# Second attention's probabilities: turned by 32x32 block transposes and a trip through device memory instead of by TensorE

## The reference, cut to what matters

```python
s = jnp.einsum('bnqhgd,bnshd->bnhgqs', q, kb).astype(jnp.float32) * HEAD_DIM ** -0.5 + bias
s = jnp.where(mask[None, :, None, None], s, -jnp.inf)
p = jax.nn.softmax(jnp.concatenate([s, sink], axis=-1), axis=-1)[..., :-1]
o = jnp.einsum('bnhgqs,bnshd->bnqhgd', p.astype(vb.dtype), vb)
return o.reshape(B, S, N_HEADS * HEAD_DIM) @ w_out
```

## Time and profile before

| | us |
|---|---|
| median of 3 runs | 2210.76 (2210.42 to 2211.42) |
| span of the profiled execution | 2209.0 |
| its own total | not listed apart from the three runs |
| TensorE busy | 2197.2 |
| VectorE busy | 1445.2 |
| ScalarE busy | 1106.9 |
| GpSimd busy | 550.7 |

### The profile page before, as it was taken

The page is one execution under the profiler, slowest core; times in us unless marked ns, Lnnn a source line. Parts: engine busy times, 40 slices in busy tenths (PEclk is TensorE's granted clock), DMA queues, the critical chain, the costliest instruction groups (busy, mean ns, idle before and its releaser), DMA issues.

```text
span 2209.0 us, 34195 instructions
## 1 busy us (share of the span) xinstructions
PE 2197.2 (99%) x11625; PEld 1878.9 (85%) x11625; DVE 1445.2 (65%) x1925; ACT 1106.9 (50%) x1654; POOL 550.7 (25%) x531
## 2 busy tenths in 40 slices
PE   9999999999999999999999999999999999999998
PEld 7888988888888888888888887888888888888887
DVE  6877765555664565555566667567785688756875
ACT  6445555453453454445455455565553455534553
POOL 3202220350240141053000033005540245403431
PEclk9999999999999999999999999999999999999999
DMA  7675335556555555556555653545555555555554
GB/s 254 232 230 163 115 128 204 170 190 208 191 190 192 189 189 192 186 192 193 187 185 179 227 171 135 193 160 188 195 188 196 192 183 192 189 195 192 186 209 149
DMA packets 118072, 414.21 MB, mean 188 GB/s; under 512 B 12896, under 2 KB 18048, under 8 KB 117472
## 3 DMA queue, kind: packets, MB, share of 16 engines
q1 hardware_dynamic: 111600, 401.37, 53.9%
q10 hardware_dynamic: 6384, 11.70, 1.7%
HBM read 409.29 MB, written 2.15 MB: 186 GB/s over the span
## 4 chain that ended last, share of the span: by engine, by line
PE 98%; DVE 1%; ACT 1%; issue 0%; DMA 0%; DVEq 0%; ACTq 0%
PE bank L486 33%; PE bank L494 17%; PE bank L543 7%; PE bank L545 7%; PE bank L544 7%; PE bank L1059 4%; PE bank L1060 4%; PE bank L1061 4%; PE bank L599 1%; PE bank L601 1%; PE bank L600 1%; PE bank L619 1%; PE bank L994 1%; PE bank L656 1%; PE bank L796 1%; PE bank L798 1%
## 5 line engine op out<-in xcount | busy, mean ns | idle before, releaser
L1100 DVE TENSOR_TENSOR wboth<-raw,wboth 128x1024 fp32r<-128x1024 f32 x756 | 982.2, 1302 | 607.8 <-ACT wboth L1802 607.1
L1802 ACT CAST wboth<-raw 128x1024 fp32r<-128x1024 f32 x756 | 790.9, 1049 | 711.5 <-PE bank L545 241.6
L486 PE MATMUL bank<-A,wboth 128*128 128x512 f32 x2928 | 705.1, 391 | 0.3 <-DVE wboth L1100 0.3
L486 PEld LDWEIGHTS bank<-A,wboth 128*128 128x128 f32 x2928 | 537.0, 188 | 104.6 <-issue 1.0
L494 PEld LDWEIGHTS bank<-A,wboth 128*128 128x128 f32 x2928 | 376.7, 191 | 14.8
L494 PE MATMUL bank<-A,wboth 128*128 128x256 f32 x2928 | 384.0, 283 | 0.0
L543 PE MATMUL bank<-wboth,H 128*128 128x512 f32 x576 | 224.6, 390 | 0.0
L545 PE MATMUL bank<-wboth,H 128*128 128x512 f32 x576 | 224.2, 389 | 0.0
L544 PE MATMUL bank<-wboth,H 128*128 128x512 f32 x576 | 224.1, 389 | 0.0
L2257 POOL TENSOR_TENSOR bias<-z,rs 128x256 f32<-128x256 f32 x64 | 75.7, 1182 | 481.2 <-DVE z L1131 391.6
L2257 POOL TENSOR_TENSOR PT<-z,rs 128x256 f32<-128x256 f32 x88 | 73.4, 835 | 465.4 <-DVE z L1131 464.8
(11 more groups left out here) (293 smaller groups left out, 2409.1 us busy)
## 6 DMA issues: line engine op xcount, KB each, us to landing
raw<-wstream SPq DMA_DIRECT2D x756, 512.0 KB, 3.3
bias<-bias_rows ACTq DMA_DIRECT2D x6, 512.0 KB, 5.4
x<-xrows ACTq DMA_DIRECT2D x1, 2048.0 KB, 10.0
bias<-grows ACTq DMA_DIRECT2D x2, 1024.0 KB, 6.1
out<-x SPq DMA_DIRECT2D x8, 256.0 KB, 2.1
x<-xT SPq DMA_DIRECT2D x7, 256.0 KB, 4.6
pA<-bias_rows ACTq DMA_DIRECT2D x2, 512.0 KB, 8.9
Sm<-grows ACTq DMA_DIRECT2D x1, 1024.0 KB, 5.8
```

The lines of the kernel that those rows point to most:

```text
L486: last = nc.tensor.matmul(bank(j)[:, :], whi[:, s, cols(i)], moving(j, k), start=(k == 0), stop=(k == K - 1))
L1100: V.tensor_tensor(wlo[:, s, :], raw[:, s, :], whi[:, s, :].bitcast(F32), ALU.subtract).then_inc(lo_ready, 1)
L1802: C.copy(whi[:, s, :], raw[:, s, :]).then_inc(hi_ready, 1)
```

## The change

The eight TensorE transposes of a block and the two copies from PSUM go. In their place, at the step where the copies stood, VectorE transposes the block's 128x1024 elements in 32x32 squares from `Sm` into one buffer `flip` (half of `kT`, free by then), ordered so that each group of 32 partitions holds rows that belong together. SyncE stores the buffer to device memory, 512 KB, waits for that to land, and fetches it back in four transfers of 128 KB, each to 32 partitions in runs of 256 elements, into one of two halves of `PT`. There the keys are on partitions, and the output matmuls read the probabilities as runs of 32 columns. SyncE does the store ahead of weight load s + 7 and the fetch ahead of load s + 8 of the stream, s being the step of the flip. The outputs move from places 10, 13, 15 to 13, 16, 18 (last pair: from 34, 36, 37 to 37, 39, 40), "hi" and "lo" with them. A flip waits until the block before has been stored; a fetch waits until the output of the block two before is done. The output projection's first 16 pieces come in another order: rows 0 to 3 of both halves, then 4 and 5 of both, then 6 and 7 of both. The bytes stored and fetched are 1 MB for each of 12 blocks.

```diff
-SWA_AT = {"score": (5, 8, 10), "turn": (9, 12, 14), "out": (10, 13, 15), "max": (6, 9, 11), "exp": (6, 9, 11), "inv": (8, 11, 13),
-          "copy": (10, 13, 15), "hi": (None, 14, 16), "lo": (None, 15, 17)}
...
+SWA_AT = {"score": (5, 8, 10), "max": (6, 9, 11), "exp": (6, 9, 11), "inv": (8, 11, 13), "flip": (10, 13, 15), "out": (13, 16, 18),
+          "hi": (None, 17, 19), "lo": (None, 18, 20)}
+SWA_AT_LAST = {"score": (29, 32, 33), "max": (30, 33, 34), "exp": (30, 33, 34), "inv": (32, 35, 35), "flip": (34, 36, 37),
+               "out": (37, 39, 40), "hi": (None, 40, 41), "lo": (None, 40, 41)}
...
+WO2_FIRST = [(f, h) for hs in ((0, 1, 2, 3), (4, 5), (6, 7)) for f in range(2) for h in hs]
+FLIP_LOAD = 7
...
+    flipped = nc.dram_tensor("flipped", [3 * PAIRS, P, 8 * P], F32).ap()
...
+        flip = kT[:, 1, :, :].rearrange("p a b -> p (a b)")[:, 0:8 * P]
...
+        def swa_probs_of(n, kt, half):
+            t = SWA_BLOCKS[n % 3][0]
+            runs = PT[:, n % 2, :, :].rearrange("p a b -> p (a b)").rearrange("p (i e b) -> p e i b", i=4, e=8)
+            return runs[:, half::2, :, :] if t == 0 else runs[:, 2 * half + kt::4, :, :]
...
+            def swa_store(n):
+                sp.wait_ge(swa["flipped"], n + 1)
+                sp.dma_start(flipped[n], flip).then_inc(swa["stored"], 16)
+            def swa_fetch(n):
+                sp.wait_ge(swa["stored"], 16 * n + 16)
+                if n >= 2:
+                    sp.wait_ge(swa["o_done"], n - 1)
+                for j in range(4):
+                    rows = flipped[n].rearrange("(i a) (j c) -> j a i c", i=4, j=4)[j]
+                    sp.dma_start(PT[32 * j:32 * j + 32, n % 2, :, :].rearrange("p a b -> p (a b)").rearrange("p (i c) -> p i c", i=4),
+                                 rows).then_inc(swa["landed"], 16)
...
+            loads(BLK, first)
+            for i in range(first, last):
+                for n in swa_due("flip", i - PB["q2"] - FLIP_LOAD - 1):
+                    swa_fetch(n)
+                for n in swa_due("flip", i - PB["q2"] - FLIP_LOAD):
+                    swa_store(n)
+                load_one(i)
+            loads(last, NPIECE // SLOTS * SLOTS)
...
-            def swa_turn(n):
-                _, t, _, _, probs = swa_block(n)
-                pe.wait_ge(swa["scaled"], n + 1)
...
-                pe.wait_ge(swa["pt_act"], n + 1)
+                pe.wait_ge(swa["landed"], 64 * n + 64)
...
-                                                PT[:, kt, e0 + half:e1:2, :], start=(kt == 0), stop=(kt == t))
+                                                swa_probs_of(n, kt, half), start=(kt == 0), stop=(kt == t))
...
-            for i, (f, h) in enumerate(WO_FIRST):
+            for i, (f, h) in enumerate(WO2_FIRST):
...
+            def swa_flip(n):
+                dve.wait_ge(swa["scaled"], n + 1)
+                if n:
+                    dve.wait_ge(swa["stored"], 16 * n)
+                V.transpose(flip.rearrange("p (j e b) -> p e j b", j=4, e=8),
+                            Sm[:, n % 3 * 8 * P:(n % 3 + 1) * 8 * P].rearrange("p (e j a) -> p e j a", e=8, j=4)).then_inc(swa["flipped"], 1)
```

More of the change, by code:

```diff
@@ L334, in program @@
             "scores", "max", "step", "shift", "sinkdiff", "exp", "sinkexp", "inverse", "scaled",
-            "turned", "pt_act", "pt_dve", "o_done", "o_hi", "o_ready")}
+            "flipped", "stored", "landed", "o_done", "o_hi", "o_ready")}
         bias_in = [sem(f"bias_in{i}") for i in range(4)]
@@ L436, in load, with loads, load_one @@
                 sp.dma_start(raw[:, s, :], wstream[ds(i, 1)].rearrange("a p n -> p (a n)")).then_inc(raw_landed[s], 16)
[L438 to L441, removed]
+            def loads(a, b):
+                with sp.Fori(a // SLOTS, b // SLOTS) as it:
+                    for j in range(SLOTS):
+                        load(it * SLOTS + j, j)
+            def load_one(i):
                 sp.wait_ge(lo_ready, i - SLOTS + 1)
                 sp.dma_start(raw[:, i % SLOTS, :], wstream[i]).then_inc(raw_landed[i % SLOTS], 16)
+            def swa_store(n):
[9 more added lines that the diff above has]
+                                 rows).then_inc(swa["landed"], 16)
+            first, last = PB["q2"] // SLOTS * SLOTS, (PB["q2"] + ATT_PIECES + FLIP_LOAD) // SLOTS * SLOTS
+            loads(BLK, first)
[6 more added lines that the diff above has]
+            loads(last, NPIECE // SLOTS * SLOTS)
+            for i in range(NPIECE // SLOTS * SLOTS, NPIECE):
+                load_one(i)
             for t in range(QT):
@@ L902, in swa_output @@
                         last = nc.tensor.matmul(psum[4 + t][c, e0 // 2 * P:e1 // 2 * P], vN[:, kt, g * P + half * HD:g * P + half * HD + HD],
[L903 to L905 removed]
+                                                swa_probs_of(n, kt, half), start=(kt == 0), stop=(kt == t))
+                last.then_inc(swa["o_done"], 1)
             def swa_after(i):
@@ L910, in swa_after @@
                     swa_output(n)
-                for n in swa_due("turn", i):
-                    swa_turn(n)
                 for n in swa_due("score", i):
@@ L1630, in _ @@
             for i in range(ATT_PIECES + 2):
-                for n in swa_due("copy", i):
-                    swa_copy(n)
+                for n in swa_due("flip", i):
+                    swa_flip(n)
                 for n in swa_due("lo", i):
@@ L2123, in square @@
                 else:
-                    act.wait_ge(piece_used, SLOTS + PB["wo2"] + (WO_FIRST.index((f, 7)) + 1 if f < 2 else 8 * f + 8))
+                    act.wait_ge(piece_used, SLOTS + PB["wo2"] + (WO2_FIRST.index((f, 7)) + 1 if f < 2 else 8 * f + 8))
                 if f:
@@ L2408, with rows_out @@
     misc = np.concatenate([gates, a["nsa_cmp_w2_k"][0], a["nsa_cmp_w2_v"][0]], axis=1)
-    def rows_out(w):
+    def rows_out(w, order_of):
         by_piece = rows(w).reshape(4, BLK, BLK, P, P)
-        first, half = zip(*WO_FIRST)
+        first, half = zip(*order_of)
         return np.concatenate([by_piece[list(first), list(half)], by_piece[2:].reshape(-1, BLK, P, P)]).reshape(-1, P, P)
     stream = [rows(vs), tiled(kc), tiled(vc), tiled(ks), tiled(kw), in_turn, misc.reshape(P, BLK, P).transpose(1, 0, 2),
-              tiled(w_in[:, :D]), rows_out(a["nsa_w_out"][0])]
+              tiled(w_in[:, :D]), rows_out(a["nsa_w_out"][0], WO_FIRST)]
     for c in range(FF_CHUNKS):
@@ L2426 @@
     sinks = a["swa_sinks_2"][0].reshape(PAIRS, 2, HPG).transpose(0, 2, 1).reshape(-1)
-    stream += [rows(swa[:, D + kv2:]), tiled(swa[:, D:D + kv2]), tiled(swa[:, :D][:, heads]), rows_out(a["swa_w_out_2"][0][heads])]
+    stream += [rows(swa[:, D + kv2:]), tiled(swa[:, D:D + kv2]), tiled(swa[:, :D][:, heads]), rows_out(a["swa_w_out_2"][0][heads], WO2_FIRST)]
     up, down = a["ffn_w_up_2"][0], a["ffn_w_down_2"][0]
```

23 lines of the change are left out of this document (5 added, 18 removed).

## The result

The changed kernel takes 2214.57 us (median of 16 executions, 2211.76 to 2218.81), the kernel before 2211.08 us (16 executions, 2210.34 to 2212.49): a ratio of 1.0017 [1.0010, 1.0024]. It is 3.5 us slower, inside the 4.4 us that were taken as no change, and 2.6 us above the range of the prediction. The profiled execution took 2212.75 us with a span of 2210.9, which answers to the 2209.0 of before.

A forecast was written before the change was run, and what follows sets the result against it. TensorE, busy 99% of the span, was taken to bound the kernel. Removed turns of 9.6 us less a 1.2 us wait gave 8.4 us off, a forecast of 2202.4 us, range 2200.6 to 2212.

The forecast's parts named there:

- The prize: On TensorE, removing 96 turns, twelve groups of eight at about 0.80 us each, saves 9.6 us.
- The turn: On VectorE, one 128x1024 transpose per block takes 1.3 us, ends 0.7 and 2.6.
- The trip in the traffic: Per block, transpose 1.3, store 3.3, fetch 4.2 and hand-overs 0.3 us: 9.1 us, ends 6.9 and 16.4.
- The trip of 9.1 fits in all of them: Covers before the output groups, 10.3 to 13.5 us, hide the trip; only block 11 waits, 1.2 us.
- Rival A: Late landings: trip 11.9 us, 6.5 us of TensorE waits, 3.1 us gained, 2207.6 us; chance 0.20.
- The places: Where TensorE waits for fetched data: block 11 alone, 1.2 us; block 10 has 10.3 us of cover.
- What moves at no cost: Later output groups, 32-column operand runs and the projection's new order cost TensorE zero; output groups stay 1.01 us.
- rival C: 32-column runs slow output groups: prize gone from 1.8 us a group, 2207 us at 1.4; chance 0.08.
- The clock: A lower granted clock after a wait, listed only as a sign of being wrong, with no size.
- The queue: SyncE's in-order queue: weight loads about 3 us late, 8.5 us to spare, hidden until the trip nears 15 us.
- rival B: Slower: output groups wait on fetches, prize spent at a trip of about 12.7 us, 2217 at 14; chance 0.14.

The follow-up runs named there:

- run without a trip: Changed kernel with VectorE transposing straight into `PT`, no store or fetches, probabilities turned only within 32x32 squares: 2201.62 us, ratio 0.9958.
- filled waits: Changed kernel with 8 and 16 matmuls that nothing reads ahead of the waits of blocks 3 and 10: 2212.60 us, ratio 1.0007.
- gain rows later: Changed kernel with the 1 MB gain-row load issued at step 42, after the last fetch landed, not at step 38: 2211.75 us, ratio 1.0004.
- both: Changed kernel with the gain-row load and the bias loads of pairs 2 and 3 both issued later: 2208.93 us, ratio 0.9995.
- bias later: Changed kernel with the bias loads of pairs 2 and 3 issued at steps 17 and 25, not beside fetches of blocks 0 and 3: 2214.22 us, ratio 1.0020.
- a buffer of its own: Changed kernel with both late loads, a separate flip buffer for block 11, its store before block 10's fetches, block 10's scores one piece earlier: 2211.13 us, ratio 1.0002.

## Why the prediction was wrong

**The prize: right, a little small.** 9.6 us was forecast. The run without a trip is 9.1 us faster while it pays 1.7 us for the reduction, so the turns were worth 10.7 or so (its trace is 9.0 us shorter over the stretch compared below).

**The turn: right.** 1.3 taken, 1.24 measured. The Trainium skill's price (VectorE: DVE Perf Modes, The three transpose paths) made it 2.5; the measurement is half of that.

**The trip in the traffic: the step that failed.** "Taken 3.3" for the store and "taken 4.2" for the fetch were measured as 4.3 and 5.3 at the median, the trip as 11.3 and not 9.1, and 14.8 and 14.2 at the two blocks that TensorE waited for. So "The trip of 9.1 fits in all of them" failed: the waits that were put at 1.2 us came to 7.4. Rival A had a trip of 11.9 and 6.5 us of waits, and the prediction argued it down with "the lines carry only 114 to 152 GB/s here". That is the second half of the stage; the first 48 us, with block 3 in them, carry 166. And it was read as if the change added no traffic. It adds 12 stores and 12 fetches of 512 KB, 12.6 MB in some 118 us, 107 GB/s: from 166 and 142 GB/s to 286 and 238, with a share of 0.88 and 0.74. With weight loads cut to a quarter the trip is 8.8 us (store 2.8, fetch 4.2). In the same step the store was priced like a weight load of the kernel before, and the fetch "nearest to the best, since SP issues little else at that time"; both leave out that the weight loads of SyncE's own queue are still in flight when a store is issued behind them: taking one of them away from in front of it gave 5.4 to 3.7 us.

**The places: wrong.** Rival A saw block 1 short in each of the first three pairs, then blocks 10 and 11; the forecast block 11 alone. The waits are at block 3, where the bias loads fall on the fetches, and at block 10, where the gain rows do. The gain rows were missing from the prediction, though the change moves them: they wait for the last turn, which is now VectorE's, and so fall into the trip (issued at 1388.21; at 1393.42 in the kernel before). Block 10 had less cover as well, 9.2 us and not 10.3. A turn was to start "when that copy does, or sooner"; the copy began 1.3 us before piece 36 ended (1386.16 and 1387.50), the turn 0.4 us after it (1381.91 and 1381.55). Block 11's own wait, 1.2 us in the forecast, doesn't show, because block 10's is in front of it.

**"What moves at no cost": half right.** The order and the 32-column operand are free (rival C falls: undisturbed output groups still take 1.01 us, as from 1384.36 to 1385.37). But taking turns and an output group away from the change of stage uncovered VectorE's last reduction, 1.7 us. Putting an output group back there left 1.6 us of it in one run and 1.1 in another. The prediction named only "the next weight piece" as late next.

**The clock: named, not priced.** A lower granted clock stood only among the signs of being wrong. The two stretches at 0.50 cost 4.0 us by the estimate above, of which the run with filled waits got 2.0 back at the median.

**The queue: right.** TensorE waits for no rounded piece in this stage.

The account of the profiled execution: 10.7 gained; 2.4 lost at block 3, 5.0 at block 10, 1.7 at the reduction, 4.0 to the clock, 13.1 in all: 2.4 us longer. From the first score group (1265.31 before, 1264.92 after) to the first piece of the output projection with f = 2 (1420.64 and 1422.54) the two traces differ by 2.3 us (155.33 and 157.62). The prize is spent at a median trip of 11.3 us, where rival B had 12.7 in every pair: the waits come from the two longest trips and not from the median one, and B's account had no clock and no reduction in it.

What stays open: the single executions of one kernel differ by several us where waits remain. Mean clock and time go together, but only one execution of each has a profile, so which wait made each of them longer isn't shown. Nor is it shown why the wait of 2.43 us at block 3 was followed by a lower clock, while waits of 2.31 and 2.62 us (the gain rows later, blocks 0 and 11) and of 2.51 (both, block 11) were not. And what the lower clock costs is an estimate from the changed kernel's trace; the run with filled waits bears out its direction alone.

## What to carry to other kernels

Add a change's own traffic to the row of the transfer engines before taking a transfer's length from it, and list every load of every queue that is in flight, or is released, within the trip. A trip that is hidden with a microsecond or two to spare isn't hidden: give it cover for its crowded length, or put the store ahead of the loads in its queue. And a wait of TensorE can cost more than its length, since the work behind it may run at half the clock: here an estimated 1.6 us on top of 2.43, and 2.4 on top of 4.97.

## What the runs showed of the hardware that was not expected

A 512 KB store behind weight loads in one queue took 5.4 us, with one load fewer ahead of it 3.7, and with those loads a quarter as long 2.8. The single fetches hardly follow (a median of 2.8 us in all three runs), but one beside a 1 MB load of the other queue took 7.9. The Trainium skill (DMA: Bandwidth & Descriptors, Queues, rings and completion order) says that each transfer engine serves the queues in turn, packet by packet; the collisions of the two queues at blocks 3 and 10 agree, and moving the loads away took both long waits down (2.43 to 0.78 at block 3, 4.97 to 0.32 at block 10). The fetches of a block show it in more than one profile: beside the gain rows block 10's took 9.2, 8.4 and 9.4 us (changed kernel, bias later, waits filled), without them 4.5 and 4.2 (gain rows later, both).

VectorE turns 128x1024 float32 in 32x32 squares in 1.24 us, less than its subtraction of as many elements.

The granted clock fell to 0.50 for 3.4 us at the end of a wait of 2.43 us, and for 6.8 us in a wait of 4.97, in a stage whose clock had been 1.00 before the change. It fell for 3.4 us in a wait of 4.17 (the bias later) and for 6.8 us in one of 4.98 (a buffer of its own), and with eight and sixteen matmuls put into the two waits it didn't fall.
